# Residual transposes between output tiles, and two gate tiles advanced together, in a hybrid decoder step

## The reference, cut to what matters

```
x = x + _rmsnorm(m @ lw['w_out'], lw['norm_post'])
x = x + jax.nn.sigmoid(x @ lw['w_ple_gate']) * (p.astype(x.dtype) @ lw['w_ple'])
```

## Time and profile before

| | us |
|---|---|
| median of 3 runs | 1336.61 |
| lowest, highest | 1335.29, 1339.57 |
| span of the profiled execution | 1342.7 |
| time of the profiled execution itself | not given |
| PE busy in it | 1271.8 (95%) |
| DVE, ACT, POOL busy | 696.4, 594.0, 246.8 |

### The profile page before, as it was taken

One profiled execution on the slowest core, in us unless ns is written; L12 is line 12 of the kernel. 1 busy time (PEld: TensorE's weight loads), 2 busy tenths in 40 slices (PEclk: granted clock), 3 DMA queues, 4 the chain that ended last, 5 costly groups with the idle time before them and its releaser, 6 DMA issues.

```text
span 1342.7 us, 22968 instructions
## 1 busy us (share of the span) xinstructions
PE 1271.8 (95%) x8596; PEld 1214.0 (90%) x8596; DVE 696.4 (52%) x967; ACT 594.0 (44%) x967; POOL 246.8 (18%) x318
## 2 busy tenths in 40 slices
PE   2899999999999999999999899999999999979996
PEld 1789999899999989999999799999999899959996
DVE  3856464745646474554637854443444334484441
ACT  4345564745556464554546233333333333344331
POOL 4422130402213040221305310000000200051221
PEclk8899999999999999999999899999999889999998
DMA  9323332333233233333225435445555835516550
GB/s 265 104 64 79 107 82 78 92 99 87 78 107 80 78 92 99 87 82 104 67 81 157 134 106 162 142 141 156 152 148 151 229 106 144 156 32 170 160 145 27
DMA packets 274054, 155.44 MB, mean 116 GB/s; under 512 B 6933, under 2 KB 269629, under 8 KB 273364
## 3 DMA queue, kind: packets, MB, share of 16 engines
q1 hardware_dynamic: 267044, 137.50, 36.1%
q0 software_dynamic: 6976, 17.48, 5.1%
HBM read 149.57 MB, written 5.61 MB: 116 GB/s over the span
## 4 chain that ended last, share of the span: by engine, by line
PE 78%; DVE 8%; ACT 5%; issue 4%; DMA 2%; SPq 1%; POOL 1%; DVEq 0%; ACTq 0%; POOLq 0%
PE acc L1409 15%; PE acc L1410 14%; PE acc L1411 14%; PE wide L1411 5%; PE wide L1409 5%; PE wide L1410 5%; PE wide L1428 4%; PE wide L1575 2%; PE wide L1561 2%; PE wide L1486 1%; DVE kf L1213 1%; PE wide L1581 1%; DVE wl L990 1%; PE wide L1528 1%; DMA wraw<-in_w_in 1%
## 5 line engine op out<-in xcount | busy, mean ns | idle before, releaser
L990 DVE TENSOR_TENSOR wl<-wraw,wh 128x1024 fp32r<-128x1024 f32 x252 | 315.5, 1256 | 229.0 <-ACT wh L672 227.6
L1409 PE MATMUL acc<-hh,wh 128*128 128x320 f32 (+1 forms) x1088 | 370.5, 340 | 6.2 <-DVE wl L990 4.1
L672 ACT CAST wh<-wraw 128x1024 fp32r<-128x1024 f32 x256 | 267.6, 1046 | 215.3 <-PE acc L1411 124.7
L1410 PE MATMUL acc<-hl,wh 128*128 128x320 f32 (+1 forms) x1088 | 339.4, 312 | 0.0
L1411 PE MATMUL acc<-hh,wl 128*128 128x320 f32 (+1 forms) x1088 | 339.0, 312 | 0.0
L1409 PEld LDWEIGHTS acc<-hh,wh 128*128 128x128 f32 x1088 | 207.1, 190 | 11.1 <-issue 4.4
L1410 PEld LDWEIGHTS acc<-hl,wh 128*128 128x128 f32 x1088 | 207.0, 190 | 3.6
L1411 PEld LDWEIGHTS acc<-hh,wl 128*128 128x128 f32 x1088 | 206.2, 190 | 0.0
L1409 PE MATMUL acc<-x1h,wh 128*128 128x320 f32 x256 | 83.7, 327 | 7.2 <-DVE x1l L1365 7.2
L1410 PE MATMUL acc<-x1l,wh 128*128 128x320 f32 x256 | 80.6, 315 | 0.0
L1411 PE MATMUL acc<-x1h,wl 128*128 128x320 f32 x256 | 80.5, 315 | 0.0
(11 more groups left out here) (351 smaller groups left out, 2466.0 us busy)
## 6 DMA issues: line engine op xcount, KB each, us to landing
wraw<-in_w_in SPq DMA_DIRECT2D x160, 512.0 KB, 3.8
wraw<-in_w_branch SPq DMA_DIRECT2D x32, 512.0 KB, 3.9
wraw<-in_w_out SPq DMA_DIRECT2D x32, 512.0 KB, 3.9
wraw<-in_w_ple_gate SPq DMA_DIRECT2D x32, 512.0 KB, 4.0
xt<-in_x_prompt SPq DMA_DIRECT2D x2, 1024.0 KB, 5.1
S0n<-in_state_wkv POOLq DMA_DIRECT2D x16, 128.0 KB, 6.3
out<-so POOLq DMA_DIRECT2D x16, 128.0 KB, 2.8
xt<-in_x_prompt POOLq DMA_DIRECT2D x2, 1024.0 KB, 7.9
```

The source lines that it names most:

```text
L672: A.copy(wh[:, slot, :], wraw[:, slot, :]).then_inc(s["hi_ready"], 1)
L990: V.tensor_tensor(wl[:, slot, :], wraw[:, slot, :], wh[:, slot, :].bitcast(F32), ALU.subtract).then_inc(s["lo_ready"], 1)
L1409: M.matmul(out[:, 0:width], wh[:, slot, wcol], hi, start=first, stop=False)
L1410: M.matmul(out[:, 0:width], wh[:, slot, wcol], lo, start=False, stop=False)
```

## The change

The 18 groups of transposes are taken out of their block and put ahead of output tiles 2 to 15, two groups ahead of each of tiles 2 to 5 and one ahead of each of the others (`TURNED`); the 14 tiles are written out instead of looped, on PE and ACT. All 16 embeddings are made early: their weights are loaded before the output tiles, into space of constants and of `t1` and `la` that are no longer used, after a wait for the last `ml`. Gate tiles 0 and 1 advance together: in round k PE makes embedding k + 4, step k of tile 0 and step k - 3 of tile 1 (LAG = 3); the first four chunks of `w_ple_gate` are loaded in the order first halves, second halves. The casts and splits of the gate chunks 3 to 6, which stood in the first two gate tiles, are placed by hand: chunk 3 ahead of the square root, chunks 4 and 5 within the rounds, chunk 6 in the second gate tile. The diff, without the list of semaphores:

```diff
--- before.py
+++ after.py
@@ -44,7 +44,8 @@
...
 PLE = 256
-EMB = 8
+EMB = KT
+LAG = 3
 BUF = 15
@@ -73,6 +74,9 @@
...
 CHUNKS = BASE_GATE + 2 * KT
+TURNED = {i: [2 * (i - 2), 2 * (i - 2) + 1] if i < 6 else [i + 2] for i in range(2, KT)}
@@ -308,7 +312,17 @@
...
         emb = at(used["ml"][0], "emb", [P, EMB, T])
-        wple0 = r4.take("wple0", [P, EMB - 2, 2 * P])
+        wple0 = r4.take("wple0", [P, 6, 2 * P])
+        wple1 = at(used["cm"][0], "wple1", [P, 6, 2 * P])
+        wple2 = at(used["t1"][0], "wple2", [P, 2, 2 * P])
+        assert used["wple1"][1] <= used["cm"][1] and used["wple2"][1] <= used["la"][1]
+        def embedding_weights(m):
+            if m < 2:
+                return wple[:, m, :]
+            if m < 8:
+                return wple0[:, m - 2, :]
+            return wple1[:, m - 8, :] if m < 14 else wple2[:, m - 14, :]
         assert r5.next <= used["gt"][1]
@@ -431,11 +445,17 @@
...
                         load(view, k0, n * (2 * P) + (m * P + col), n * (2 * CH_MERGE) + BASE_MERGE, CH_MERGE * m + j)
-            for view, start in ((wo_v, BASE_OUT), (wg_v, BASE_GATE)):
-                with sp.Fori(0, KT // 2) as n:
-                    for m in range(2):
-                        for h in range(2):
-                            load(view, KC * h, n * (2 * P) + m * P, n * 4 + start, 2 * m + h)
+            with sp.Fori(0, KT // 2) as n:
+                for m in range(2):
+                    for h in range(2):
+                        load(wo_v, KC * h, n * (2 * P) + m * P, n * 4 + BASE_OUT, 2 * m + h)
+            for h in range(2):
+                for m in range(2):
+                    load(wg_v, KC * h, m * P, BASE_GATE, 2 * h + m)
+            with sp.Fori(1, KT // 2) as n:
+                for m in range(2):
+                    for h in range(2):
+                        load(wg_v, KC * h, n * (2 * P) + m * P, n * 4 + BASE_GATE, 2 * m + h)
@@ -620,9 +640,9 @@
...
             pool.dma_start(pt[0:NB * TB, 2, :], p_sample[0].rearrange("b t d -> (b t) d")).then_inc(s["x2_in"], 16)
+            pool.wait_ge(s["ml_ready"], KT)
             for m in range(EMB):
-                to = wple[:, m, :] if m < 2 else wple0[:, m - 2, :]
-                pool.dma_start(to.rearrange("p (k n) -> p k n", k=2),
+                pool.dma_start(embedding_weights(m).rearrange("p (k n) -> p k n", k=2),
                                wple_v[:, :, m * P:(m + 1) * P]).then_inc(s["map_in"], 16)
@@ -640,21 +660,9 @@
...
-            pool.wait_ge(s["ple_ps"], 2)
-            for m in range(2):
-                pool.dma_start(wple[:, m, :].rearrange("p (k n) -> p k n", k=2),
-                               wple_v[:, :, (EMB + m) * P:(EMB + m + 1) * P]).then_inc(s[f"wple_in{m}"], 16)
-            with pool.Fori(0, EMB // 2) as n:
+            with pool.Fori(0, KT // 2) as n:
                 for m in range(2):
                     store(n, m)
-            with pool.Fori(EMB // 2, KT // 2 - 1) as n:
-                for m in range(2):
-                    wait_alone("ple_ps", n * 2 + m + 1)
-                    pool.dma_start(wple[:, m, :].rearrange("p (k n) -> p k n", k=2),
-                                   wple_v[:, :, ds(n * (2 * P) + (m + 2) * P, P)]).then_inc(s[f"wple_in{m}"], 16)
-                    store(n, m)
-            for m in range(2):
-                store(KT // 2 - 1, m)
             pool.wait_ge(s["y_out0"], 16 * KT)
@@ -918,30 +926,44 @@
...
+            def turned_tile(u):
+                if u < KT:
+                    act.wait_ge(s["xT_ps"], u + 1)
+                    A.copy(xT[:, T * u:T * (u + 1)], B[u % 4][:, 0:T]).then_inc(s["xT_ready"], 1)
+                else:
+                    act.wait_ge(s["pT_ps"], u - KT + 1)
+                    A.copy(pT[:, u - KT, :], B[4 + u - KT][:, 0:T]).then_inc(s["xT_ready"], 1)
             for m in range(2):
                 square_tile(0, m)
-            for k in range(KT):
-                act.wait_ge(s["xT_ps"], k + 1)
-                A.copy(xT[:, T * k:T * (k + 1)], B[k % 4][:, 0:T]).then_inc(s["xT_ready"], 1)
-            for k in range(2):
-                act.wait_ge(s["pT_ps"], k + 1)
-                A.copy(pT[:, k, :], B[4 + k][:, 0:T]).then_inc(s["xT_ready"], 1)
-            with act.Fori(1, KT // 2) as n:
-                for m in range(2):
-                    act.wait_ge(s["sacc_ready"], n * 2 + m - 1)
-                    square_tile(n, m)
+            for i in range(2, KT):
+                act.wait_ge(s["sacc_ready"], i - 1)
+                for u in TURNED[i]:
+                    turned_tile(u)
+                square_tile(i // 2, i % 2)
+            def gate_ahead(j):
+                ahead(BASE_GATE, BASE_GATE // SLOTS, j)
+            gate_ahead(0)
             act.wait_ge(s["sacc_ready"], KT)
...
             for k in range(KT):
-                if k < EMB:
-                    act.wait_ge(s["ple_ps"], k + 1)
-                    A.copy(emb[:, k, :], B[k % 4][:, 0:T]).then_inc(s["emb_done"], 1)
+                act.wait_ge(s["ple_ps"], k + 1)
+                A.copy(emb[:, k, :], B[k % 4][:, 0:T]).then_inc(s["emb_done"], 1)
                 act.wait_ge(s["x1b"], k + 1)
                 A.copy(x1h[:, T * k:T * (k + 1)], xT[:, T * k:T * (k + 1)]).then_inc(s["x1h_ready"], 1)
+                if k in (10, 13):
+                    gate_ahead(1 if k == 10 else 2)
+            def first_gate(m):
+                if m:
+                    gate_ahead(3)
+                act.wait_ge(s["chunk_used"], BASE_GATE + 3 + m)
+                A.activation(g3[:, m, :], acc[m][:, 0:T], ACT.Sigmoid).then_inc(s["g3_ready"], 1)
@@ -959,8 +981,8 @@
...
-            gate_tile(0, 0)
-            gate_tile(0, 1)
+            first_gate(0)
+            first_gate(1)
             token_tile(0, 0)
@@ -1355,6 +1377,10 @@
...
+            def gate_ahead(j):
+                ahead(BASE_GATE, j)
+            gate_ahead(0)
             dve.wait_ge(s["srt"], 1)
@@ -1369,30 +1395,30 @@
...
                     lower_part(k - 3)
+                if k in (12, 15):
+                    gate_ahead(1 if k == 12 else 2)
             for k in range(KT - 3, KT):
...
-            def gate_tile(n, m, early=False, last=False):
+            def gate_tile(n, m, first=False, last=False):
                 i = n * 2 + m
                 for h in range(2):
-                    if not last or 2 * m + h + AHEAD < 4:
+                    if first:
+                        if m == 1 and h == 1:
+                            gate_ahead(3)
+                    elif not last or 2 * m + h + AHEAD < 4:
                         ahead(n * 4 + BASE_GATE, 2 * m + h)
                 dve.wait_ge(s["g3_ready"], i + 1)
-                if early:
-                    e = emb[:, :, :].rearrange("p k t -> p (k t)")[:, ds(n * (2 * T) + m * T, T)]
-                else:
-                    dve.wait_ge(s["ple_ps"], i + 1)
-                    e = B[m][:, 0:T]
+                e = emb[:, :, :].rearrange("p k t -> p (k t)")[:, ds(n * (2 * T) + m * T, T)]
                 V.tensor_tensor(g3[:, m, :], g3[:, m, :], e, ALU.mult).then_inc(s["g3m"], 1)
...
             dve.wait_ge(s["emb_done"], EMB)
-            with dve.Fori(0, EMB // 2) as n:
-                for m in range(2):
-                    gate_tile(n, m, early=True)
-            with dve.Fori(EMB // 2, KT // 2 - 1) as n:
+            for m in range(2):
+                gate_tile(0, m, first=True)
+            with dve.Fori(1, KT // 2 - 1) as n:
                 for m in range(2):
@@ -1738,37 +1764,33 @@
...
             sizes = (P, P, NB * TB)
+            def turned_tile(u):
+                if u < KT:
+                    if u >= 4:
+                        pe.wait_ge(s["xT_ready"], u - 3)
+                    for t in range(3):
+                        last = transpose(B[u % 4][:, P * t:P * t + sizes[t]], xt2[0:sizes[t], t, P * u:P * (u + 1)])
+                    last.then_inc(s["xT_ps"], 1)
+                else:
+                    k = u - KT
+                    for t in range(3):
+                        last = transpose(B[4 + k][:, P * t:P * t + sizes[t]], pt[0:sizes[t], t, P * k:P * (k + 1)])
+                    last.then_inc(s["pT_ps"], 1)
             pe.wait_ge(s["x2_in"], 96)
-            for k in range(KT):
-                if k >= 4:
-                    pe.wait_ge(s["xT_ready"], k - 3)
-                for t in range(3):
-                    last = transpose(B[k % 4][:, P * t:P * t + sizes[t]], xt2[0:sizes[t], t, P * k:P * (k + 1)])
-                last.then_inc(s["xT_ps"], 1)
-            pe.wait_ge(s["x2_in"], 96)
-            for k in range(2):
-                for t in range(3):
-                    last = transpose(B[4 + k][:, P * t:P * t + sizes[t]], pt[0:sizes[t], t, P * k:P * (k + 1)])
-                last.then_inc(s["pT_ps"], 1)
-            with pe.Fori(1, KT // 2) as n:
-                for m in range(2):
-                    out_tile(n, m, True)
+            for i in range(2, KT):
```

(63 more changed lines are left out.)

## The result

| us | before | changed |
|---|---|---|
| median | 1337.87 (10 executions) | 1328.28 (10) |
| lowest, highest | 1335.29, 1349.47 | 1324.9, 1330.44 |
| span and mean granted clock of the profiled execution | 1342.7, 0.974 | 1323.3, 0.986 |

The medians are 9.6 us apart. The ratio over all executions is 0.9912, 95% interval 0.9889 to 0.9935, which is 11.8 us: faster, but about half of the 22.0 that was forecast (1314.6 as a time), and outside the range of 1310.5 to 1321.0. The unchanged kernel shows two kinds of execution, most between 1334 and 1340 us with a mean clock of 0.979 or more, about one in four between 1342 and 1349 with 0.974 to 0.977, and the profile that I forecast from (0.974) was of the second kind, while the changed kernel's profile is the fastest of its ten.

The account below looks back on a forecast made before the run. PE, busy 95% of the span, was taken as the bound, with two low-clock holes. Terms -10.3 - 3.1 - 8.6 = -22.0 us took the median of 1336.6 to 1314.6; own range 1311.8 to 1317.6, with rivals and spread 1310.5 to 1321.0.

Parts of the forecast that it names:

- block and the low clock behind it: Before output tile 2: removing the transposes' block saves 15.2 us, and the half-rate clock it leaves for tile 2 1.9.
- slots: Ahead of output tiles 2 to 15: 18 transpose groups in 14 slots add 6.8 us, bounds 5.8 and 10.3.
- Residual's transposes: Output stage: block and low clock removed, slots added, -15.2 - 1.9 + 6.8 = -10.3 us (-6.8 to -11.3).
- differences carry over: Whole kernel: the -22.0 us against the 1342.7 profiled span applies equally to the median, 6.1 us lower, giving 1314.6.
- the slots are dear: Rival, output stage: every group costs 0.57 as dense work drains before and after; 3.5 us more, 1318.1; chance 0.12.
- The weights behind POOL's loads: Output stage: extra embedding loads delay w_out chunk 7 to 1071.0 to 1076.3; no stall taken, bound 0.4 or 3 us.
- Ahead of the square root: Before the gates: casting gate chunk 3 ahead of the table load moves the real Sqrt later, +0.6 us.
- First two gate tiles: Gate start: two tiles advance together in 1.96 us rounds, PE the bound, clock 1.00; -3.1 us including the 0.6.
- clock dips once more: Rival, gate stretch: the clock dips again for 10 us, half of it lost, giving 1319.6; chance 0.12.
- Late gate tiles: Later gate tiles: eight embeddings leave saturated tiles, 8 x 1.08 = -8.6 us.
- Slower, or no change: Outcomes: slower, the clock staying at 0.50 through both stretches' successors, 1342.7, chance 0.03; same, within 0.3%, chance 0.02.
- doesn't do what it says: Rival: embeddings only move into a stretch growing as much, slots cost what the block did; within 0.3%; chance 0.02.

Follow-up runs that it names:

- before again: The unchanged kernel, run and profiled a second time with no edit: 1339.19 us, ratio 1.0018.
- spreading alone: The kernel before with only the transposes spread ahead of the written-out output tiles, nothing else of the diff: 1338.78 us, ratio 0.9996.
- widened kernel: The changed kernel with the third transpose of each of the 18 groups over all 128 rows instead of 64: 1321.41 us, ratio 0.9873.
- the kernel with idle time and block: Changed gates only, transposes kept in their block, against which x's loads were held back by one chunk of weights: 1337.24 us.
- the widened block: Changed gates only, transposes kept in their block, with the third transposes widened to 128 rows: 1323.24 us, ratio 0.9887.

## Why the prediction was wrong

The direction was right and the mechanism of most terms too; the sum was twice the gain. Step by step:

| term | forecast | measured |
|---|---|---|
| block and the low clock behind it | -17.1 | -10.3 (before again); -17.1 only in one execution of four |
| slots | +6.8 | +10.9 |
| start of gates, cast ahead of the Sqrt in it | -3.1 | -2.95 |
| late embeddings | -8.6 | -8.1 |
| sum | -22.0 | -10.5 (the whole: -9.6 by the medians, -11.8 by the ratio) |

- **Residual's transposes, the block: mis-sized by 6.8.** This is the step that failed, together with the sentence under the sum that differences carry over. I saw that the span stood 6.1 us above the median and took the gap for something that the change leaves alone, although the rows show a clock of 0.50 in the block. (The gap was larger still: in every other run the time is 1.6 us over the span, so this execution took some 1344.3, 7.7 over the median.) The earlier trace rows showed the first groups 0.57 apart, before the clock fell, so that the block at full clock could be worked out as 18 x 0.57 = 10.3: 6.8 less than what I removed, which is most of that gap. The two numbers side by side would have told it. Together with the slots, the step "Residual's transposes" was forecast at -10.3 and measured +0.6 by the traces, and spreading alone gave no gain in the median.
- **The slots: mis-sized by 4.1.** I priced a single group by the token group "since ten slots look just like the token slots". They did not: the earlier trace rows had 0.17 us of issue ahead of the 64-row weight load, and a token group has no such load. The widened kernel shows the 0.32 once that load is gone. Adding 0.17 to the 0.32 and to the 0.57 would not have been right either: a double slot measured 1.19, a single one 0.61, so each group costs about 0.6. The rival "the slots are dear", all groups at 0.57, was the closest thing on record to the truth (10.3), at a chance of 0.12. It was right in the sum and not in its reason, dense work that drains: the widened kernel has the same dense work around its slots. By itself it gave 1318.1.
- **The weights behind POOL's loads: right.** Chunk 7 was ready at 1073.5. This trace runs 1.6 us ahead of before's at the square of tile 1 (1060.74 for 1062.37), so on before's scale that is 1075.1, in the later part of the 1071.0 to 1076.3 forecast, and there was no stall. The queues in 1060 to 1064 of the changed kernel (packets, MB, share of 16 engines) moved packet for packet, as in the earlier trace rows:

```profile
q0 software_dynamic: 352, 0.95, 84.2%
q1 hardware_dynamic: 352, 0.18, 20.3%
```

  That agrees once more with what the Trainium skill says of taking turns packet by packet (DMA: Bandwidth & Descriptors, Queues, rings and completion order).
- **Ahead of the square root: right.** PE's first step stands 9.67 us behind the last square, 9.30 before: +0.37 for +0.6.
- **First two gate tiles: right** (the recorded "to 1310.3" is 1210.3, by its own sum), in time (36.14 for 39.09), in the 1.95 us of a round and in the clock. The rival "clock dips once more" did happen, in a smaller form: five of the ten traces with changed gates have a dip of a few us around the first rounds, and their gates take 37.8 us, not 36.14. It costs 1.7, not 5.
- **Late gate tiles: right.** The tiles give back 7.5 us, and the end behind the last sigmoid 0.6 of its 1.08.
- **Slower, or no change**: neither came. The lower end of the range's own sum is 1314.6 - 1.0 - 2 = 1311.6, not 1311.8, which changes nothing. Half of "doesn't do what it says" holds: the slots cost what the block did, in the median.

What of the clock? The Trainium skill (TensorE: Matmul & The Clock Gate, Part 4: PE-mode transpose) says that transposes don't count as PE work for the clock. The 16.4 us at 0.50 in the kernel with idle time and block agree with that; 18.36 us of nothing but transposes at 1.00 speak against it in its strict form, and the measurement decides. The clock fell as well in the sparse rounds of before's first gate tile, and it came back under dense matmuls. The three blocks behind dense work or less than 1 us of idle time kept 1.00, and the one behind 4.32 us kept the 0.50 to which the clock had fallen in the wait. Two traces show that a block does not always keep the level that it finds. In the profile before PE began again at 1063.60 at full clock, and the clock fell some 2 us into the transposes, with PE busy all the time:

```profile
1064.00:1065.00 1.00, 1.00 (x7) 0.64 (x6) 0.00 (x0) 0.58 (x2) 0.00 (x0) 1.00 1.05 292
1065.00:1066.00 1.00, 1.00 (x7) 0.54 (x5) 0.00 (x0) 0.70 (x2) 0.00 (x0) 0.84 1.03 274
1066.00:1067.00 1.00, 1.00 (x5) 0.55 (x5) 0.00 (x0) 0.43 (x1) 0.00 (x0) 0.50 1.16 280
```

And the widened block, behind 1.85 us, fell soon after it began and was back at 1.00 before it ended; that the wider weight loads helped it is possible and wasn't tried. Why a gap of 1 to 2 us brings the fall in some executions and not in others is open: the link between idle time and low clock is shown for 4 us, and for the gap of before it is argued from that and from the counts.

## What to carry to other kernels

When the profiled execution stands off the median, look for the gap in it before pricing anything, first where the granted clock is low: what is only there in that execution is not in the median, and removing it buys a narrower spread. Price an operation by a row of the same shape: a transpose of 64 rows is not a cheaper one of 128, and widening it to unused rows was worth 6.3 us, where all the rest of the change gave about 10. Behind a wait, dense matmuls are better than a block of transposes: after the same wait of some 4 us the clock was back 5 us after PE began with the first (two groups of transposes, then matmuls), and 21.7 us after with the second.

## What the hardware did that I had not expected

- A weight load of 64 rows waits 0.17 us for issue where one of 128 rows does not: widening 18 of them gave 3.3 us in a block (1326.51 to 1323.24) and about 5 us spread between dense matmuls (slots of 10.9 to 5.8 us; the stage went from 110.39 to 104.55, with 0.7 of it from a wait for `pt` that the second trace doesn't have).
- 96 float32 transposes in a row leave the granted clock at 1.00; 54 behind 4.32 us of idle time run at 0.50 to their end.
- The same code holds two levels of time: of 71 executions of before, 53 have a median of 1336.6 us and 18 one of 1345.5. In the one trace of the slower kind the low clock in and behind the block accounts for 6.8 of the 8.9.
